# Remainders of the last query block: twelve of them move from VectorE to GpSimd, with six row gathers between them

## What is computed

```python
q = (xt @ wq).reshape(-1, PEER_HEADS, 2, PEER_HALF)        # wq is 2048 x 2048
s = jnp.einsum('thpc,hpnc->thpn', q, keys)                 # 8 heads, 2 sides, 128 keys
sv, si = lax.top_k(s, PEER_TOPK)                           # 16 best on each side
cand = sv[:, :, 0, :, None] + sv[:, :, 1, None, :]         # 256 pairs
top_s, top_j = lax.top_k(cand, PEER_TOPK)                  # 16 best pairs: 128 picks a token
ue = jnp.take(u, eid, axis=0)                              # one row of 2048 a pick
act = gelu(jnp.einsum('thkd,td->thk', ue, xt))
ve = jnp.take(v, eid, axis=0)
out = jnp.einsum('thk,thkd->td', gate * act, ve)
```

## Time and profile before

| | us |
|---|---|
| median of 3 executions | 2961.72 |
| lowest and highest | 2961.16 and 2962.39 |
| the profiled execution | 2965.63 |
| its span, first to last instruction | 2963.9 |
| PE busy | 2339.0 |
| DVE busy | 2035.8 |
| ACT busy | 1120.3 |
| POOL busy | 819.3 |

### The profile page before, as it was taken

How to read it: one execution, slowest core, us unless ns; L and a number is a source line. 1 busy time by engine, 2 the same in 40 slices (tenths; PEclk the granted TensorE clock), 3 DMA queues, 4 the chain that set the end, 5 groups by cost and what they waited for, 6 DMA issues and landing times.

```text
span 2963.9 us, 29163 instructions
## 1 busy us (share of the span) xinstructions
PE 2339.0 (79%) x10495; PEld 1848.7 (62%) x10495; DVE 2035.8 (69%) x2513; ACT 1120.3 (38%) x1257; POOL 819.3 (28%) x646
## 2 busy tenths in 40 slices
PE   9999999999999999999999990000022249998997
PEld 7888888888888888888888770000011136555654
DVE  5456554554544565745665678999999888887888
ACT  5444344444444554444344442211222244222222
POOL 1000000000000000000000017888887875554553
PEclk9999999999999999999999995555555559999998
DMA  8666556666666546555566469999999967999997
GB/s 281 207 187 193 168 179 189 183 194 188 184 191 185 169 137 206 159 175 170 171 186 224 160 219 403 415 416 417 417 404 397 416 284 297 408 408 388 408 407 301
DMA packets 165304, 792.14 MB, mean 267 GB/s; under 512 B 20188, under 2 KB 20240, under 8 KB 131248
## 3 DMA queue, kind: packets, MB, share of 16 engines
q1 hardware_dynamic: 105344, 390.12, 41.0%
q0 software_dynamic: 59824, 400.23, 33.4%
HBM read 788.17 MB, written 2.10 MB: 267 GB/s over the span
## 4 chain that ended last, share of the span: by engine, by line
PE 58%; DVE 18%; DMA 13%; issue 6%; POOL 3%; ACT 1%; POOLq 0%; SPq 0%; DVEq 0%; ACTq 0%
PE banks L751 53%; DMA v_rows<-in_peer_v_rest,eid 10%; DVE ring L2224 9%; DVE banks L2298 3%; DMA ring<-in_peer_u,eid 3%; POOL ring L676 2%; PE banks L789 1%; PE banks L1135 1%; DVE v_split L2309 1%; POOL v_rows L718 1%; POOL ring L685 1%; PE banks L763 1%; DVE onehots L2203 0%; DVE cand L2127 0%; PE banks L838 0%
## 5 line engine op out<-in xcount | busy, mean ns | idle before, releaser
L751 PE MATMUL banks<-w_split,xT 128*128 128x512 f32 x7008 | 1611.6, 391 | 6.4 <-DVE xT L1631 5.4
L751 PEld LDWEIGHTS banks<-w_split,xT 128*128 128x128 f32 x7008 | 1314.2, 188 | 279.9 <-DVE xT L1631 6.1
L1584 DVE TENSOR_TENSOR w_split<-w_raw,w_split 128x1024 fp32r<-128x1024 f32 x592 | 722.3, 1224 | 733.2 <-ACT w_split L1198 732.0
L1198 ACT ACTIVATE w_split<-w_raw 128x1024 fp32r<-128x1024 f32 x592 | 626.5, 1059 | 913.4 <-PE banks L751 874.5
L2224 DVE CUSTOM_DVE_ANT_0 ring<-ring,banks 128x2048 f32<-128x2048 f32 x194 | 438.5, 2284 | 48.0 <-DMA ring<-in_peer_u,eid 44.1
L2298 DVE SCALAR_TENSOR_TENSOR banks<-v_rows,wgt,banks 128x896 f32<-128x896 f32 x254 | 292.9, 1153 | 67.8 <-DMA v_rows<-in_peer_v_rest,eid 66.5
L676 POOL DMA_INDIRECT ring<-in_peer_u,eid x256 | 245.4, 959 | 257.9 <-DVE eid L2156 157.8
L718 POOL DMA_INDIRECT v_rows<-in_peer_v_rest,eid x256 | 245.6, 959 | 233.2 <-DVE banks L2298 196.7
L1166 PE MATMUL banks<-v_raw,wT 128*128 128x512 f32 (+1 forms) x1024 | 298.9, 435 | 0.7 <-ACT wT L1494 0.7
L1135 PE MATMUL banks<-onehots 128*128 128x128 f32 x512 | 103.7, 370 | 245.1 <-DVE onehots L2203 233.8
L611 POOL DMA_DIRECT2D row_a<-in_final_g x1 | 0.5, 534 | 1063.3 <-DVE ao L1846 1063.3
(11 more groups left out here) (322 smaller groups left out, 1341.3 us busy)
## 6 DMA issues: line engine op xcount, KB each, us to landing
w_raw<-in_a_w_in SPq DMA_DIRECT2D x192, 512.0 KB, 3.6
v_raw<-in_peer_v_dense SPq DMA_DIRECT2D x128, 576.0 KB, 7.9
w_raw<-in_b_w_in SPq DMA_DIRECT2D x128, 512.0 KB, 3.5
w_raw<-in_w_in SPq DMA_DIRECT2D x112, 512.0 KB, 3.6
w_raw<-in_a_w_out SPq DMA_DIRECT2D x64, 512.0 KB, 4.3
w_raw<-in_b_w_out SPq DMA_DIRECT2D x32, 512.0 KB, 3.9
w_raw<-in_w_out SPq DMA_DIRECT2D x32, 512.0 KB, 4.5
w_raw<-in_peer_wq SPq DMA_DIRECT2D x32, 512.0 KB, 3.7
```

The source lines that it names most:

```text
L751: last = mm(ps[half][:, 2 * t + n, :], xt[:, xp, kk, tok], w_split[:, s, wp, n * BANK:(n + 1) * BANK], start=(k == 0 and xp == 0 and wp == ...
L1198: fn(w_split[:, k % SPLIT_SLOTS, 0, :], w_raw[:, k % RAW_SLOTS, :], ACT.Copy).then_inc(hi_done, 1)
L1584: v.tensor_tensor(w_split[:, s, 1, :], w_raw[:, k % RAW_SLOTS, :], w_split[:, s, 0, :].bitcast(F32), ALU.subtract).then_inc(split_done, 1)
```

## The change

POOL forms the remainders of chunks 4 to 15 of `peer_q1`, and DVE none in that block (`held=KT`). They count on a semaphore of their own, `split_by_pool`; PE and SP wait for the one or the other by chunk number (`is_split`), and SP's loads of the two query blocks are written out in place of a loop. POOL's program becomes: remainders 4 to 10, gathers 0 and 1, remainder 11, gathers 2 and 3, remainder 12, gathers 4 and 5, remainders 13, 14 and 15, then gathers 6 to 9.

```diff
+POOL_AHEAD = 4
...
+        split_by_pool = sem("split_by_pool")
...
+        POOL_FROM = FIRST["peer_q1"] + POOL_AHEAD
+
+        def is_split(eng, i):
+
+            if i < POOL_FROM:
+                eng.wait_ge(split_done, i + 1)
+            else:
+                eng.wait_ge(split_by_pool, i + 1 - POOL_FROM)
...
-            load_pairs(peer_wq_2[0], "peer_q", 0, 1)
+            for n in range(2):
+                for k in range(KT):
+                    is_split(sp, FIRST[f"peer_q{n}"] + k - RAW_SLOTS)
+                    sp.dma_start(w_raw[:, k % RAW_SLOTS, :], peer_wq_2[0][k * P:(k + 1) * P, n * COLS:(n + 1) * COLS])\
+                        .then_inc(raw_landed[k % RAW_SLOTS], 16)
...
-            for r in range(FIRST_ROWS):
+            def split_lo(k):
+
+                pool.wait_ge(hi_done, FIRST["peer_q1"] + (k + 1))
+                s = k % SPLIT_SLOTS
+                nc.gpsimd.tensor_tensor(w_split[:, s, 1, :], w_raw[:, k % RAW_SLOTS, :], w_split[:, s, 0, :].bitcast(F32),
+                                        ALU.subtract).then_inc(split_by_pool, 1)
+
+            for k in range(POOL_AHEAD, 11):
+                split_lo(k)
+            for r in range(EARLY_ROWS):
+                gather_u(r)
+                if r % 2:
+                    split_lo(11 + r // 2)
+            for k in range(11 + EARLY_ROWS // 2, KT):
+                split_lo(k)
+            for r in range(EARLY_ROWS, FIRST_ROWS):
                 gather_u(r)
...
-                    pe.wait_ge(split_done, c + (k + 1))
+                    is_split(pe, c + k)
...
-                                    10: second[5:7], 11: second[7:]}, last=True)
+                                    10: second[5:7], 11: second[7:]}, last=True, held=KT)
```

## The result

| | before | after |
|---|---|---|
| median of 20 executions each, us | 2962.66 | 2966.91 |
| lowest and highest, us | 2958.95 and 2967.90 | 2962.21 and 2971.95 |
| span of the profiled execution, us | 2963.9 | 2967.2 |

The change costs 4.25 us between the medians. The ratio is 1.0012, with an interval of 1.0006 to 1.0017: slower, beyond doubt, but by less than 0.2%. The forecast was +4.0.

A forecast was written before the change was run, and what follows sets the result against it. The prediction took PE's end of chunk 15 in the last query block, then a transfer-filled stage, as the bound. Some 0.9 us of waiting removed and 4.9 added gave +4.0 on 2961.72: 2965.7 us, range 2960.8 to 2971.0.

The forecast's parts named there:

- The step that carried it: From PE's end of chunk 15 in the last query block: any shift there reaches the kernel's end one to one.
- What quicker remainders could give back: PE's waits for VectorE's remainders before chunks 14 and 15, 0.56 and 0.36 us: at most 0.92 us to gain.
- two pauses of 2.5 us: PE in the last query block waits 2.5 us for GpSimd's remainders before each of chunks 12 and 13.
- The clock: Rival: PE's granted clock falls in its pauses, the last three chunks take 5.4 each, +8 more, 2973.9 us; chance 0.05.
- signs of being wrong: Picks at 1745, a remainder over 2.6 us, block and kernel ends moving differently, or the clock falling in PE's pauses.
- Queue and holding: GpSimd remainders 11 to 15 stand behind gathers awaiting picks; GpSimd and VectorE block each other, ending the first group near 1750.7.
- gathers that run free: Last query block, by the Trainium skill: VectorE's two-input instructions do not delay gathers; sum +2.9 instead of +4.0 us.
- the walk: Last query block stepped through in time, GpSimd and VectorE delaying each other; PE ends at 1775.1 against 1771.1, +4.0 us.
- Covers: Slack around the last query block: 5 us for chunk 15's load, 5 us for the second group before the dot products.
- No holding: Rival: GpSimd and VectorE do not block each other, picks come at 1744.7, block end +0.7, 2962.4 us; chance 0.10.
- A dearer remainder: Rival: GpSimd's remainder takes 2.6 us or more, not 2.35; +6.9 at 2.7, +9.0 at 3.0; chance 0.14, including more blocking.
- A gain above 0.2%: Rival: less stands in the way in the 635 us after the block, about 2952 us; chance 0.05.

The follow-up runs named there:

- the kernel with all twelve ahead of the gathers: Changed kernel, but GpSimd forms the remainders of chunks 4 to 15 first and only then issues the gathers; ratio to the kernel before 1.0011.
- the kernel with seven on GpSimd: Changed kernel, but GpSimd forms only remainders 4 to 10, VectorE 11 to 15, with no remainder behind the gathers; median 2961.48 us, ratio to before 0.9994.
- the kernel that adds holding alone: Kernel before, plus seven GpSimd subtractions of 128x1024 that nobody waits for, each after the rounding of chunks 4 to 10; ratio to before 1.0021.
- the kernel with the last five on GpSimd: Changed kernel, but VectorE forms the remainders of chunks 4 to 10 and GpSimd only 11 to 15, between the gathers; ratio to before 1.0020.

## Why the prediction was right

**The step that carried it.** The block's end, and with it the first dot product, moved by 4.06 and 4.05, and the medians by 4.25; 4.0 was forecast. That such a shift reaches the end one to one agrees with these numbers, but the interval of the changed kernel's ratio alone runs from 1.8 to 5.0 us, and the kernel with all twelve ahead of the gathers shows that the block's end is not all that counts: its block is 1.1 shorter and its median 3.8 longer than before. The stretch from the block's end to the start of the last gather, forecast as unchanged, was 638.1 before (1771.09 to 2409.17) and 639.4 after (1773.46 to 2412.86).

**What quicker remainders could give back.** Put at 0.92, measured 1.10 (47.77 less 46.67). The forecast read the pauses off the idle times in the earlier trace rows, which count from the overlapping end of the products before; by starts the first is 1765.13 - 1739.83 - 9 x 2.72 = 0.82, not 0.56.

**The sum was right by two errors that cancel.** Forecast were two pauses of 2.5 us before chunks 12 and 13 and a steady clock. They came before the same chunks, but were 1.42 and 2.09, 1.5 less together, and the half clock added 1.65. The pauses were shorter because chunk 13's remainder was ready 41.7 after the rounding of chunk 4 (1763.34 - 1721.63), where the forecast has 43.3. The picks came at 26.5, not 27.4: the first group was held by 5.2 us in four instructions, not by 6.0. And the gathers were not held; they took 0.95 to 1.03, where some 0.3 had been added for three of them. The clock was among the rivals, with the whole rest of the block at half speed, +8 and a chance of 0.05; it fell for about 3 us and cost a fifth of that. The forecast named a fall of the clock in the pauses among its signs of being wrong, and in the profiled execution that sign came. Queue and holding came as forecast; that the total agrees to 0.1 us is luck.

**The gathers.** The sum that the forecast read out of the Trainium skill (SBUF — State Buffer, "SBUF: two separate sides"), with gathers that run free, was nearer in this term, but not for its reason. It is put at +2.9; by the walk's own terms, with chunk 13 at 1765.8, it is +3.1. And it is not a rule that they run free: with VectorE's 1.22 us remainders beside them, in the kernel with seven on GpSimd, the first gather took 1.56 and the last of the six 1.68. In the changed kernel those remainders are gone, and beside VectorE's shorter two-input instructions a gather took 1.03 at most; elsewhere such an instruction held one too, as in the kernel before, where the gather at 1771.87 took 1.37 while L2150 ran (1771.73, 0.69). The forecast had carried the held gathers of the earlier trace rows over to a stretch in which what held them had been removed.

**Who goes first.** The walk let the two engines take turns. In the first group they did: L2180 (2.77, above) got in between chunk 9's remainder and chunk 10's, and chunk 10's took 2.85. Later they did not: L2176, begun during chunk 13's remainder, waited 6.44 us, through chunks 14's and 15's too. This favoured PE, since no remainder of the last three stood behind VectorE for long (7.03 for three).

**Covers.** Chunk 15's load landed just before 1761.75, 40.1 after the rounding of chunk 4 (40.9 at worst was forecast), and its rounding was over before GpSimd came to it, so the cover held with some 3 us. The second group ended at 1770.68, 6.7 before the first dot product needed VectorE.

**Rivals.** No holding: falls, by the kernel that adds holding alone, and in the changed kernel by the picks at 26.5 where that rival has 21.4 (1744.7 less 1723.32). A dearer remainder: 2.40, not 2.35, nowhere near the 2.6 at which it would have decided. A gain above 0.2%: none; even the best split of the work moves the block by 1.1 us.

## What to carry to other kernels

Work moved to an idle engine takes its place in that engine's queue: price the instructions that stand ahead of it, and their waits, before its own duration. The same eleven chunks run without a pause when the remainders go ahead of the gathers and when the gathers have no remainder behind them; only the mixture stalls. Where two engines hold each other up, work that nobody waits for costs too: seven spare GpSimd subtractions lengthened the block by 5.8 us.

## What the runs showed of the hardware that was not expected

A VectorE instruction with two SBUF inputs that meets a GpSimd subtraction can wait for several of them in a row: 6.44 us for an instruction of 0.19, over three subtractions that followed each other without a gap, and 6.46 in the kernel with the last five on GpSimd. Between chunks 9's and 10's remainders it got in; what decides stays open. PE's granted clock fell to 0.50 within the block after pauses of 1.42 and 2.09 us with a chunk between them, and did not fall there in another kernel after pauses of 1.20, 2.03 and 2.10; what decides between the two stays open too.
